# A decoder step with 32 experts on one core: float32 row gather by a stationary selection, the residual added in the second half of the output projection, the down bias added once

## What is computed

```
h = rms_norm(x, norm_mix); p = h @ w_in
y_a = rwkv7_mix(p[..., :SHIFT_COLS], ...)        # 8 heads x 64, delta-rule scan, group norm, gate
y_b = conv_mix(p[..., SHIFT_COLS:], ...)         # GLU, causal depthwise conv of 31 taps, layer norm, swish
x = x + concat(y_a, y_b) @ w_out
h2 = rms_norm(x, norm_ffn)
logits = h2 @ w_router + b_router                # top 4 of 32, softmax over the four
gt = min(xe @ w_gate[e] + b_gate[e], 7)
up = clip(xe @ w_up[e] + b_up[e], -7, 7)
y  = ((up + 1) * gt * sigmoid(1.702 * gt)) @ w_down[e] + b_down[e]
x = x + sum over the token's experts of gate * y
out = rms_norm(x, norm_final)
```

## Time and profile before

| | |
|---|---|
| median of 3 runs | 1287.1 us (1282.87 to 1288.11) |
| profiled execution, its own time | 1292.66 us |
| its span | 1290.8 us |
| PE busy in the span | 1217.9 us (94%) |
| DVE, ACT, POOL busy | 500.5, 172.0, 63.6 us |
| mean granted TensorE clock | 0.977 |
| read from HBM | 424.80 MB |

### The profile page before, as it was taken

How to read it: one execution, slowest core, us unless ns; L and a number is a source line. 1 busy time by engine, 2 the same in 40 slices (tenths; PEclk the granted TensorE clock), 3 DMA queues, 4 the chain that set the end, 5 groups by cost and what they waited for, 6 DMA issues and landing times.

```text
span 1290.8 us, 24922 instructions
## 1 busy us (share of the span) xinstructions
PE 1217.9 (94%) x10245; PEld 605.9 (47%) x10245; DVE 500.5 (39%) x1104; ACT 172.0 (13%) x341; POOL 63.6 (5%) x103
## 2 busy tenths in 40 slices
PE   7999799999999999999999999999999999999995
PEld 5667589856533343333433433333433333333332
DVE  5758653232462234232332333322332233332324
ACT  2352123112300000000000000000000000000001
POOL 0214350010000000000000000000000000000000
PEclk9999899989799999999999999999999999999998
DMA  9321300185599999999999999999999999999994
GB/s 263 110 68 43 110 32 4 42 284 199 208 421 365 422 422 422 421 422 422 422 422 422 422 422 422 421 422 422 422 422 422 422 422 421 422 422 422 421 421 170
DMA packets 81970, 428.80 MB, mean 332 GB/s; under 512 B 15775, under 2 KB 30031, under 8 KB 32766
## 3 DMA queue, kind: packets, MB, share of 16 engines
q1 hardware_dynamic: 80490, 428.00, 82.0%
q10 hardware_dynamic: 1436, 0.16, 0.1%
HBM read 424.80 MB, written 3.11 MB: 331 GB/s over the span
## 4 chain that ended last, share of the span: by engine, by line
PE 41%; DMA 34%; DVE 3%; SPq 1%; ACT 1%; issue 1%; DVEq 0%
DMA arena<-in_w_up_dram 33%; PE bank L1662 28%; PE bank L1703 3%; PE bank L1639 3%; PE bank L1550 2%; PE bank L1595 1%; SPq L1352 1%; PE bank L1668 1%; PE bank L1710 1%; PE bank L1685 1%; ACT arena L1512 1%; DMA arena<-in_x_sample_dram 1%; DVE arena L1941 0%; PE bank L1554 0%; PE bank L1647 0%
## 5 line engine op out<-in xcount | busy, mean ns | idle before, releaser
L1662 PE MATMUL bank<-ring,arena 128*64 128x512 f32 x2048 | 458.2, 600 | 17.5 <-ACT arena L1512 17.5
L1662 PEld LDWEIGHTS bank<-ring,arena 128*64 128x64 f32 x2048 | 145.0, 138 | 305.9 <-issue 300.7
L1662 PE MATMUL bank<-arena 128*64 128x512 f32 x1024 | 232.4, 595 | 11.9 <-DMA arena<-in_w_up_dram 11.8
L1662 PEld LDWEIGHTS bank<-arena 128*64 128x64 f32 x1024 | 69.7, 136 | 163.2 <-issue 115.1
L1941 DVE TENSOR_TENSOR arena<-arena,bank 128x512 f32<-128x512 f32 (+1 forms) x192 | 117.3, 678 | 0.0
L510 PE MATMUL bank<-arena,ring 128*128 128x336 f32 x352 | 103.7, 452 | 1.1 <-DVE arena L644 1.1
L1639 PEld LDWEIGHTS bank<-arena 128*128 128x128 bf16 (+1 forms) x2304 | 77.6, 99 | 41.6 <-issue 39.5
L1841 DVE TENSOR_SCALAR arena<-arena 96x64 bf16<-96x64 f32 x33 | 8.3, 251 | 226.2 <-PE bank L1668 226.2
L1703 PE MATMUL bank<-arena 64*128 64x512 f32 (+1 forms) x384 | 91.2, 606 | 0.0
L1929 DVE TENSOR_SCALAR arena<-bank 128x512 f32<-128x512 f32 x32 | 22.1, 691 | 173.9 <-PE bank L1668 173.9
L1639 PE MATMUL bank<-arena 128*128 128x64 bf16 (+1 forms) x2304 | 85.3, 194 | 1.4 <-DVE arena L1829 1.4
(11 more groups left out here) (359 smaller groups left out, 910.9 us busy)
## 6 DMA issues: line engine op xcount, KB each, us to landing
ring<-in_w_gate_dram SPq DMA_DIRECT2D x128, 1024.0 KB, 22.9
arena<-in_w_up_dram SPq DMA_DIRECT2D x128, 1024.0 KB, 25.8
ring<-in_w_down_dram SPq DMA_DIRECT2D x128, 1024.0 KB, 24.9
ring<-in_w_in_dram SPq DMA_DIRECT2D x11, 1024.0 KB, 5.2
ring<-in_w_out_dram SPq DMA_DIRECT2D x4, 1024.0 KB, 8.0
arena<-in_x_prompt_dram SPq DMA_DIRECT2D x2, 512.0 KB, 5.1
out_wkv_sample_dram<-arena SPq DMA_DIRECT2D x4, 256.0 KB
arena<-in_x_prompt_dram SPq DMA_DIRECT2D x2, 448.0 KB, 4.2
```

The lines of the kernel that those rows point to most:

```text
L1662: mm = M.matmul(bank[64 * hb:64 * hb + 64, b, :], tokens(cc), w[:, c, 512 * hb:512 * hb + 512], start=(cc == 0), stop=False)
```

## The change

- Stage 1: 15 convolution steps that stood behind two DVE products now stand before them. The product of `bonT` and `vT` moves from the end of stage 1 to the head of DVE's stage 2.
- Output projection: the first half is `zT` alone. The three residual matmuls of each block move to the second half, and with them the wait for `x_in`. The variance stands after block 1, the inverse root after block 3. The wait for `heads_ready` moves behind block 1.
- The 24 transposes back to rows are parted: twelve (blocks 0 to 3) stand between blocks 6 and 7 of the second half, twelve where all stood. ACT copies the first ones between its squares. The third of the first twelve reuses bank 6 and waits for ACT's copy of the first.
- Gather: the selection (64 columns) is stationary and the rows move, 512 columns at a time: six float32 matmuls (`gather`) put the rows of 64 slots into bank 5. ACT copies them (`take_rows`), PE turns them by four transposes (`turn`), and DVE multiplies once (`take_x`). The whole gather stands between the up product and the activation's transposes. ACT makes `h`, the rows times their norm factor in float32, once. The three bf16 parts, `gather_scale` and their DVE and ACT instructions are gone.
- Down bias: the two bias matmuls of each down product are gone. In the first body the transposed gate weights `gT32` times `b_down` are added by six more matmuls of the combine.
- DMAs: `norm_ffn` in four DMAs of 256 elements for one of 512, the bias split over two matrices for three, `b_down` as one plain load.

The core of the diff:

```diff
-                convolve(6)
+                convolve(21)
                 dve.wait_ge(R["kk_sq"], 4)
...
-                convolve(8)
                 dve.wait_ge(R["exp_ready"], 4)
                 link(V.tensor_tensor(kT, kT, emL, ALU.mult))
-                convolve(7)
                 convolve(2)
...
-                dve.wait_ge(R["shifted"], NBA)
-                dve.wait_ge(R["rk_read"], 4)
-                V.tensor_tensor(bonT, bonT, vT, ALU.mult)
...
                 V.tensor_tensor(seq4, seqrow[:, 0:4], seqrow[:, 4:8], ALU.add).then_inc(S["seq4_ready"], 1)
+                V.tensor_tensor(bonT, bonT, vT, ALU.mult)
...
                 for d in range(KC):
                     act.wait_ge(F["x2_ready"], d + 1)
                     if d == 4:
                         act.wait_ge(F["ssq_done"], 1)
                     A.activation(xsq[:, d % 4, :], x2T[:, d, :], ACT.Square).then_inc(F["xsq_ready"], 1)
+                    if d >= 5:
+                        take_acc(0, d - 5)
...
-                def body(n):
+                for i, (t0, n) in enumerate(TILES):
+                    A.activation(h[0:n, i, :], acc[0:n, i, :], ACT.Identity, scale=small[0:n, 28 + i:29 + i])\
+                        .then_inc(F["h_ready"], 1)
+
+                def body(n, first=False):
                     act.wait_ge(F["t1_ready"], n + 1)
                     A.activation(sg, t1, ACT.Sigmoid, scale=ALPHA).then_inc(F["sg_ready"], 1)
+                    take_rows(n + 1)
...
-                pe.wait_ge(F["heads_ready"], 1)
                 for j in range(4):
                     M.matmul(bank[:, 4 + j, 0:NT], headones, yT[:, j, :], start=True, stop=True)\
                         .then_inc(F["ymean_done"], 1)
-                pe.wait_ge(F["x_in"], 16 * 5)
...
                     if d == 6:
+                        turn_rows(0)
                 router(1)
+                pe.wait_ge(F["acc_ready"], 3)
...
-                def gather(chunks):
-                    for c in chunks:
-                        for k, part in enumerate((hi, mid, lo)):
-                            for i, (t0, m) in enumerate(TILES):
-                                mm = M.matmul(bank[:, 5, C * c:C * c + C], chunk_cols(part[0:m, i, :], c), Pm[0:m, i, :],
-                                              start=(k == 0 and i == 0), stop=(k == 2 and i == 2))
+                def gather(rows, sel):
+                    for i, (t0, m) in enumerate(TILES):
+                        for hb in range(2):
+                            mm = M.matmul(bank[64 * hb:64 * hb + 64, 5, :], sel[0:m, i, :],
+                                          rows[0:m, i, 512 * hb:512 * hb + 512], start=(i == 0), stop=(i == 2))
+                    mm.then_inc(F["gat_done"], 1)
...
-                    gather(range(0, 6))
+                    gather(h, Pm)
                     pe.wait_ge(F["act_ready"], n + 1)
...
-                    product(n, 8, 2, lambda cc: aT[:, cc % 4, cc // 4, :], 2).then_inc(F["y_done"], 1)
-                    gather(range(6, 8))
-                    gather_scale().then_inc(F["x_done"], 1)
-
+                    product(n, 8, 2, lambda cc: aT[:, cc % 4, cc // 4, :], 2)
+                    pe.wait_ge(F["xg_ready"], n + 2)
+                    turn(xg).then_inc(F["x_done"], 1)
+                    if first:
+                        for i, (t0, m) in enumerate(TILES):
+                            mm = M.transpose(bank[0:NE, 5, t0:t0 + m], gates[0:m, i, :], ident[0:m, 0:m])
+                        mm.then_inc(F["gt_turned"], 1)
...
+                            if first:
+                                mm = M.matmul(o, gT32[0:NE, t0:t0 + m], bdown[0:NE, 512 * hb:512 * hb + 512],
+                                              start=False, stop=True)
```

More of the change, by code:

```diff
@@ L129, in build @@
         bias_at = cursor[0]
-        bias3 = take(3, DM, dt=BF16)
+        bias2 = take(2, DM, dt=BF16)
+        cursor[0] = bias_at + 3 * CA
         expert_row = take(NE)
@@ L1395, in _ @@
                     .then_inc(out_stored, 16)
[L1396 removed]
+                for i, nm in enumerate(("b_gate", "b_up")):
                     for q in range(4):
@@ L1478, in _, with take_acc @@
                     .then_inc(F["yroot_ready"], 1)
-                for d in range(1, KC):
+                for d in range(2, KC):
                     take_z(d)
+                def take_acc(hb, i):
+                    n = TILES[i][1]
+                    act.wait_ge(F["acc_turned"], 3 * hb + i + 1)
+                    A.copy(acc[0:n, i, 512 * hb:512 * hb + 512], bank[0:n, ACC_BANKS[hb][i], :])\
+                        .then_inc(F["acc_ready"], 1)
                 for d in range(KC):
@@ L1585, in router, with turn_rows @@
                     mm.then_inc(F["ssq_done"], 1)
+                def turn_rows(hb):
+                    for i, (t0, n) in enumerate(TILES):
+                        if hb == 0 and i == 2:
+                            pe.wait_ge(F["acc_ready"], 1)
+                        for c in range(4):
+                            mm = M.transpose(bank[0:n, ACC_BANKS[hb][i], c * P:c * P + P], x2T[:, 4 * hb + c, t0:t0 + n],
+                                             ident)
+                        mm.then_inc(F["acc_turned"], 1)
                 pe.wait_ge(F["yT_ready"], 4)
                 pe.wait_ge(F["zp_copied"], 1)
+                pe.wait_ge(F["x_in"], 16 * 5)
                 for d in range(KC):
@@ L1595, in _ @@
                         mm = M.matmul(bank[:, d % 4, 0:NT], out_rows(cc)[:, P * d:P * d + P], yT[:, cc, :],
-                                      start=(cc == 0), stop=(cc == 3))
-                        if d == KC - 1 and cc == 1:
+                                      start=(cc == 0), stop=False)
+                        if (d, cc) in ((0, 0), (KC - 1, 1)):
                             mm.then_inc(unit_used, 1)
+                    for i, (t0, n) in enumerate(TILES):
+                        mm = M.matmul(bank[:, d % 4, t0:t0 + n], acc[0:n, i, P * d:P * d + P], ident[0:n, 0:n],
+                                      start=False, stop=(i == 2))
                     mm.then_inc(F["xy_done"], 1)
@@ L1706, in _ @@
                 pe.wait_ge(F["p_ready"], 1)
                 pe.wait_ge(F["acc_ready"], 6)
-                for c in range(KC):
-                    for i, (t0, m) in enumerate(TILES):
-                        mm = M.matmul(bank[:, (5, 2)[c // 4], C * c:C * c + C], chunk_cols(acc[0:m, i, :], c), Pm0[0:m, i, :],
-                                      start=(i == 0), stop=(i == 2))
-                    if c % 4 == 3:
-                        mm.then_inc(F["x_done"], 1)
+                gather(acc, Pm0)
```

200 lines of the change are left out of this document (81 added, 119 removed).

## The result

The changed kernel takes **1297.1 us** (median of 8 runs, 1293.3 to 1300.9) against 1288.7 of the kernel before (8 runs, 1282.9 to 1291.6): ratio 1.0069, 95% interval 1.0047 to 1.0091. I had forecast 1278.5, with 1272.5 to 1284.5 as range. The prediction is wrong, in sign too. The profiled execution has a span of 1294.4 (before 1290.8); it stands at the changed kernel's median, while the one of before stands 4 us above its own.

The account below looks back on a forecast made before the run. The weight stream at about 422 GB/s bounds the kernel, its start set by PE's path. Front -7.5, first body and table -0.7, tail -0.4 sum to -8.6 us: 1287.1 becomes 1278.5, range 1272.5 to 1284.5.

Parts of the forecast that it names:

- The step that failed: First body: six more float32 combine matmuls cost +3.1 us; with the table net -0.7, bounds +3.4 and -2.
- four passes for float32: Gather: rival that a float32 matmul is four passes, period 31.7 us, time 1348; chance 0.01.
- three signs: Prediction wrong if PE is the chain throughout near the end, period exceeds 29.3, or first gate product starts after 330.
- Stage 1, -1.5: Stage 1: moved convolution steps cost 0, bounds 0 and +0.9; moving the bonus product into a DVE wait saves 1.5 us.
- Head of stage 3, -3.4: Output projection: waits -3.1, clock -2.3, transposes +1.8, DVE's small instructions +0.2; sum -3.4 us.
- First gather, -2.6: Before the first gate product: the new gather path takes 7.0 us for 9.67, so -2.6, bounds -1.6 and -5.
- my case of full clock: First gather with PE at full clock: 5.0 us in sum, against 8.0 at half clock.
- Start of the stream: First gate product 7.5 us earlier, near 326, and with it the stream; SP issues expert 1 near 329.5.
- Loop: Expert loop: PE's period grows +0.4 to 29.0 us from 28.6, staying under the stream's 29.8.
- The table: At expert 2's selection: PE's waits shrink from about 3 to 0.7 us, and the low clock behind them should not come.
- Tail -0.4, SP 0: End of kernel: gather +0.8, bias -0.4, earlier DVE adds, net -0.4 us; SP's queue held up to 16 us, costing 0.
- the first rival: The front gives less: 4 to 5 us instead of 7.5, or 3.4 come back; time 1282.6, chance 0.23.

Follow-up runs that it names:

- rows64: Changed kernel with its down-bias matmuls, still in turns with the combine's, padded with zero rows to 64 array rows; 1286.2 us, one run.
- grouped128: Changed kernel with the six down-bias matmuls first, padded with zero rows to 128, then the six combine matmuls; 1289.0 us, ratio to before 1.0000.
- rows128: Changed kernel with its down-bias matmuls, still in turns with the combine's, padded with zero rows to all 128 array rows; 1289.2 us, one run.
- grouped: Changed kernel with the six down-bias matmuls of 32 rows first, then the six combine matmuls, instead of in turns; 1292.1 us, ratio to before 1.0021.
- oldbias: Changed kernel with b_down again split in three bfloat16 parts and added in every expert's down product; 1282.9 us, ratio to before 0.9952.
- nobias: Changed kernel with b_down left out altogether; 1280.2 us, ratio to before 0.9942.
- stage1_old: oldbias with the convolution steps and the bonus product of stage 1 back in their old places; 1283.8 us, ratio to before 0.9967.
- head_waits: oldbias with PE's waits for head constants and residual input back ahead of the means and the projection; 1290.4 us, ratio to before 0.9999.
- quad: Changed kernel with the six down-bias matmuls first, spread over the four quarters of the array's rows; 1284.5 us, ratio to before 0.9959.

## Why the prediction was wrong

**The step that failed** is the first body: "The combine has six more float32 matmuls ... twice the records of 2.78 us and 0.5, so +3.1". It took 2.78 us for six matmuls as the price of each, 0.46. That is the price of one of a pair: six with 64 rows, alternately in the lower and the upper half. The six new ones stand between them in 32 rows, so no matmul has a partner beside it. That holds even where the rows don't meet: the bias matmul at 349.54 uses rows 0 to 31 and the combine matmul behind it rows 64 to 127 and another bank, and it still started only 1.06 us later.

The runs divide the 21.2 us like this. Twelve matmuls in pairs would take 5.4 (rows64). Alone, at 0.90 each (5.40 for six in grouped128), they take 10.8, so lost pairs are 5.4. In turns with a change of rows each takes 1.05, twelve 12.5 (rows128), so the changes are 1.7, some 0.15 each. (Rates of 128 rows are used here for 32; the first matmuls of the changed kernel, at full clock, took the same 1.05.) The clock does the rest: 21.2 - 12.5 = 8.7, and 2.6 more in the gate product behind. In grouped as in the changed kernel it fell to 0.50 about 2 us after the first bias matmul that works in one quarter of the rows; in rows128 and grouped128, with bias matmuls of 128 rows, it stayed at 1.00 through combines of 12.5 and 8.3 us. That is what the rows show; what the clock follows isn't separated further.

The Trainium skill has both parts under "TensorEngine Tiling (Array Packing)" (Key Properties): different tiles of the array can work in parallel, and "Mode switching requires drain". Both agree with the trace: six matmuls in four quarters took 1.99 us where six alone took 5.40, and a change of the row count costs about 0.15 us. The prediction didn't weigh them. I also said that four passes for float32 disagree with the trace. They don't: a matmul alone takes 0.86 to 0.90, four times the 0.219 per record by which I judged. My own rows could have told me: eight records on the full array with 336 columns took 4.85 us at 0.50, so 0.30 each at full clock, more than the 0.219 of a record with 512 columns. So the Trainium skill's four passes ("FP8 and Floating Point Precision", TensorE Precision Notes) agree with these times. The gather is still cheap (2.58 us) because its halves are paired.

None of the three signs by which the prediction was to be known as wrong appeared: the chain ends on the DMAs, the period is 29.14, and the first gate starts at 319.84. All three look at the front and the loop, and no rival named the first combine; its widest bound was +3.4. Four slips in the written sums changed nothing of this: 2.78 and 0.5 are 3.3 and not 3.1; the head constants are asked for behind 8 matmuls (16 records), not 16; clock and gather both at their bounds give -2.7 more, not -4.7; and 29.8 - 8/29 is 29.5, where 29.0 + 8/29 gives the 29.3.

The rest by its steps:
- **Stage 1, -1.5.** Stage 2 starts 2.75 earlier in the trace (149.14 for 151.89), of which the bonus product explains 1.5; in oldbias and nobias, with the same stage 1, it starts at 150.66 and 150.63, near the forecast 150.3. Whether the convolution steps are worth exactly 0 isn't shown: the last of them ends at 148.0 here and at 149.3 before, but in oldbias only 0.4 ahead of stage1_old. In time stage1_old gave 0.8 to 1.9, unresolved.
- **Head of stage 3, -3.4.** Right in kind and about right in size: the two waits and the clock behind them are worth 6 us by head_waits against 5.4. From the barrier (252.1 now, 256.1 before) to the start of the gather the trace has 62.6 us for 67.6, -5.0. The clock is at full level from 256 on, earlier than the 260.5 that I expected.
- **First gather, -2.6.** 5.15 us from its start to the gate for 9.67: -4.5, my case of full clock. But in eleven of the twelve experiments its 12 records took 4.2 to 5.4 us instead of 2.8, at the low clock in part, which makes 6.5 to 8.1 from its start to the gate: the forecast's 7.0 lies among them.
- **Start of the stream.** The first gate at 319.84 for a forecast 326. In the profiles of the ten experiments with the same head it starts between 320.65 and 326.2, so the 13.5 us of this one profile are beyond the fortunate end, and the forecast is at the other. Yet this profile stands at its kernel's median; why its front is the earliest stays open.
- **Loop.** Period 29.14 for 29.0; that step was right. With the old down bias 29.35, and PE leads to the end.
- **The table.** Said to shrink. PE no longer waits for it in the changed kernel, because PE itself was 18 us late; nobias and oldbias each have a wait of 1.1 us before the gather and one of 0.5 behind it.
- **Tail -0.4, SP 0.** From the last w_up to the end of the span 31.0 us for 30.8: no gain. The four small DMAs of norm_ffn held SP for 6.2 us, under the bound of 16, and delayed nothing.

Without the failed step the sum is right in sign and too large: -8.6 less the 3.1 would be about -11.7 for no bias matmuls at all. nobias measured -7.5 (interval -10.3 to -4.5, which leaves -11.7 out), and oldbias -6.2. So front and stream gave some 4 us less than claimed, as the first rival has it; the waits of 1.1 and 0.5 at the table and the low clock in the gather are part of that, and the rest isn't divided. And one term of +3.1 was +20: first gate to last down product is 949.9 us in the changed kernel and 929.7 in nobias (1251.88 - 322.23). Of these 20, 17 show in the time; the first gate of nobias's profile starts 2.4 us later.

## What to carry to other kernels

A mean duration of a float32 matmul from a trace holds only with its neighbours. Look at how many array rows and columns it uses and whether the next one uses another half; price a new one at the lone rate (here 0.9 us, not 0.45) unless it has a partner in another half or quarter. Don't mix row counts in turns on PE's path; if a term with few rows must be added, group it and spread it over all quarters of the rows, as quad does (1.99 us for six). And a work item that is done once isn't cheap for that reason: taken out of every expert, where most of it was hidden, and put on the path of the first one, the down bias cost 17 us to save PE 0.2 per expert.

## What the runs showed of the hardware

- Float32 matmuls with 512 moving columns: 0.90 us each alone (128 rows), 0.45 in two halves of the rows, 0.33 in four quarters (1.99 for six), all at clock 1.00. About 0.15 us more for each change of the row count. Three in one half and then three in the other took 3.78 us together, 2.85 strictly in turns.
- The granted clock fell from 1.00 to 0.50 while PE was busy without a gap, about 2 us after the first float32 matmul of 32 rows in one quarter (grouped and the changed kernel); with zero rows up to 128 it stayed at 1.00 (grouped128, rows128). In the changed kernel it came back at about 375, some 5 us after the gate product had started (0.86 is the mean from 374 to 378).
- The start of the first gate differs by 6 us between profiles of kernels with the same head of stage 3, more than several of the terms that I summed; a term of 1 to 2 us there can't be read from one profile.
